# Operand addresses of a full-rate matmul: activation halves at 192 or 64 bytes from the weights, modulo 256

## What is computed

```python
def swiglu(h, w_gate_up, w_down):
    gate, up = jnp.split(h @ w_gate_up, 2, axis=-1)
    return (jax.nn.silu(gate) * up) @ w_down

def ffn_sublayer(h, shift, scale, gate, g, w_in, w_out):
    hn = modulate(rmsnorm(h, g), shift, scale)
    a, b = jnp.split(hn @ w_in, 2, axis=-1)
    y = (jax.nn.silu(a) * b) @ w_out
    return h + 0.5 * gate[:, None, :] * y
```

## Time and profile before

| | us |
|---|---|
| median of three runs | 1629.48 (1628.14 to 1629.67) |
| the profiled execution | 1628.01 |
| its span, first to last instruction | 1626.2 |
| PE busy in the span | 1593.3 (98%) |
| DVE busy | 1041.7 (64%) |
| ACT busy | 826.4 (51%) |

### The profile page before, as it was taken

How to read it: one execution, slowest core, us unless ns; L and a number is a source line. 1 busy time by engine, 2 the same in 40 slices (tenths; PEclk the granted TensorE clock), 3 DMA queues, 4 the chain that set the end, 5 groups by cost and what they waited for, 6 DMA issues and landing times.

```text
span 1626.2 us, 24165 instructions
## 1 busy us (share of the span) xinstructions
PE 1593.3 (98%) x10017; PEld 1403.6 (86%) x10017; DVE 1041.7 (64%) x1705; ACT 826.4 (51%) x1191; POOL 153.2 (9%) x141
## 2 busy tenths in 40 slices
PE   7999999999999999999999999999999999999998
PEld 6878888887889988888899999889888888789986
DVE  5786766655645577776665666557747876655554
ACT  4565544443569854444354464444544546354442
POOL 2220010100002200101001100001000000101000
PEclk9999999999999999999999999999999999999999
DMA  9756867777663365556555576598663565575552
GB/s 330 244 200 228 272 217 229 248 251 246 220 209 106 126 195 183 185 198 212 181 182 181 183 153 184 182 181 175 137 158 64 137 171 172 188 252 179 182 190 78
DMA packets 224412, 309.31 MB, mean 190 GB/s; under 512 B 5004, under 2 KB 146720, under 8 KB 224304
## 3 DMA queue, kind: packets, MB, share of 16 engines
q1 hardware_dynamic: 222208, 301.48, 60.8%
q0 software_dynamic: 1664, 5.84, 1.1%
q10 hardware_dynamic: 432, 0.45, 0.1%
HBM read 306.71 MB, written 1.05 MB: 189 GB/s over the span
## 4 chain that ended last, share of the span: by engine, by line
PE 86%; DVE 8%; ACT 4%; issue 2%; DMA 1%; ACTq 0%; DVEq 0%
PE ps L137 84%; DVE wl L150 3%; PE ps L140 2%; DVE SM L160 1%; DVE MT L160 1%; ACT wh L146 1%; ACT L146 1%; ACT SA L147 1%; ACT SA L146 1%; DMA raw<-in_a_w_qkv_dram 0%; ACT FT L146 0%; DVE MT L157 0%; DMA X<-in_x_dram 0%; DVE X L160 0%; DVE MT L150 0%
## 5 line engine op out<-in xcount | busy, mean ns | idle before, releaser
L150 DVE TENSOR_TENSOR wl<-raw,wh 128x1024 fp32r<-128x1024 f32 x498 | 611.8, 1268 | 378.7 <-ACT wh L146 378.1
L146 ACT ACTIVATE wh<-raw 128x1024 fp32r<-128x1024 f32 x498 | 501.4, 1052 | 200.9 <-PE ps L137 111.5
L137 PE MATMUL ps<-XT,wh 128*128 128x256 f32 (+1 forms) x2496 | 570.6, 315 | 2.7 <-issue 1.9
L137 PE MATMUL ps<-XT,wl 128*128 128x256 f32 x1600 | 449.0, 281 | 1.4 <-DVE wl L150 1.4
L137 PEld LDWEIGHTS ps<-XT,wh 128*128 128x128 f32 x2496 | 408.5, 189 | 43.4 <-issue 10.8
L137 PEld LDWEIGHTS ps<-XT,wl 128*128 128x128 f32 x1600 | 301.9, 189 | 2.3 <-DVE wl L150 2.0
L137 PE MATMUL ps<-wh,XR 128*128 128x512 f32 x640 | 200.5, 394 | 0.0
L137 PE MATMUL ps<-XU,wh 128*128 128x256 f32 x832 | 149.6, 282 | 0.9 <-issue 0.5
L137 PEld LDWEIGHTS ps<-wh,XR 128*128 128x128 f32 x640 | 119.6, 188 | 24.9 <-issue 0.5
L137 PE MATMUL ps<-wh,HTH 128*128 128x512 f32 x352 | 137.4, 390 | 0.0
L137 PE MATMUL ps<-wl,HTH 128*128 128x512 f32 x352 | 137.0, 389 | 0.0
(11 more groups left out here) (304 smaller groups left out, 1855.6 us busy)
## 6 DMA issues: line engine op xcount, KB each, us to landing
raw<-in_w_ffn_in_dram SPq DMA_DIRECT2D x66, 1024.0 KB, 5.1
raw<-in_ffn_w_gate_up_dram SPq DMA_DIRECT2D x44, 1024.0 KB, 5.2
raw<-in_w_in_dram SPq DMA_DIRECT2D x40, 1024.0 KB, 8.4
raw<-in_w_ada_dram SPq DMA_DIRECT2D x36, 1024.0 KB, 6.2
raw<-in_w_ffn_out_dram SPq DMA_DIRECT2D x30, 1024.0 KB, 5.0
raw<-in_ffn_w_down_dram SPq DMA_DIRECT2D x20, 1024.0 KB, 5.0
raw<-in_a_w_qkv_dram SPq DMA_DIRECT2D x12, 1024.0 KB, 7.3
raw<-in_kv_w_dram SPq DMA_DIRECT2D x8, 1024.0 KB, 6.2
```

Source lines behind the costliest of these rows:

```text
L137: return NOTHING if self.e is None else self.e.matmul(o, l, r, start=start, stop=stop, skip_group_check=skip)
L146: return self.e.activation(o, i, fn, bias=bias, scale=scale)
L150: return NOTHING if self.e is None else self.e.tensor_tensor(o, a, b, f)
```

## The change

No instruction is added, taken away or moved. Each activation gets a tile of its own over the same two regions (`XP[name]`, read through `head(name)` for H and `tail(name)` for L), with an offset by how it is used: 192 where it streams at all (`h0`, `f0`, `hk`, `hq`, `f1`, `e`, `hm`, `l`, `c1`, `c2`), 64 where it is only loaded (`ha`, `ho`, `hh`, `hb`, `hw`). `HTH`/`HTL` and `HCH`/`HCL` move from 0 to 64. The weights stay at 0. Behind the first region everything moves by 96 bytes: `C` from 64 to 160, `MT` to `SG` and the attention tiles from 128 to 224; `XC` moves from 160 to 0.

```diff
-        XR = at("XR", [P, 2, 8, T], xt0, F32R)
-        XT = at("XT", [P, 2, 8, T], xt0 + 160, F32R)
-        XRH, XRL = XR[:, 0, :, :], XR[:, 1, :, :]
-        XTH, XTL = XT[:, 0, :, :], XT[:, 1, :, :]
-        fixed.o += 2 * 8 * T * 4 + 160
+        MAIN_AT = dict(h0=192, ha=64, f0=192, hk=192, hq=192, ho=64, f1=192, e=192, hm=192, hh=64, l=192)
+        CTX_AT = dict(c1=192, c2=192, hb=64, hw=64)
+        XP = {n: at("XP" + n, [P, 2, 8, T], xt0 + d, F32R) for n, d in MAIN_AT.items()}
+        fixed.o += 2 * 8 * T * 4 + 256
...
-        f_ = Region(r0 + 384, r1)
+        f_ = Region(r0 + 352, r1)
         HTH = f_("HTH", [P, NF, T], F32R)
         HTL = f_("HTL", [P, NF, T], F32R)
...
-        XU = at("XU", [P, 2, 8, T], c_.o, F32R)
-        XV = at("XV", [P, 2, 8, T], c_.o + 352, F32R)
-        XUH, XUL = XU[:, 0, :, :], XU[:, 1, :, :]
-        XVH, XVL = XV[:, 0, :, :], XV[:, 1, :, :]
-        c_.o += 2 * 8 * T * 4 + 352
+        XP.update({n: at("XP" + n, [P, 2, 8, T], c_.o + d, F32R) for n, d in CTX_AT.items()})
+
+        def head(n):
+            return XP[n][:, 0, :, :]
+
+        def tail(n):
+            return XP[n][:, 1, :, :]
+
+        c_.o += 2 * 8 * T * 4 + 256
         r2 = c_.o
+        c_.o += 64
         HCH = c_("HCH", [P, 8, T], F32R)
         HCL = c_("HCL", [P, 8, T], F32R)
...
-                to_halves("ha", XRH, XRL, const(AB[:, 33:34]))
+                to_halves("ha", head("ha"), tail("ha"), const(AB[:, 33:34]))
```

More of the change, by code:

```diff
@@ L799, in block2_ffn @@
                 own_first[0] = False
-                for q, _ in enumerate(hidden(n, w_in, XTH, XTL, half_ready(n), range(11))):
+                for q, _ in enumerate(hidden(n, w_in, head(n), tail(n), half_ready(n), range(11))):
                     if q in GATE_PE:
@@ L905, in main @@
                 yield None
-                values = rows("av", wqkv, 2048, XTH, XTL, 8, half_ready("h0"), lambda t, n0: (a_out, "av", t, n0))
+                values = rows("av", wqkv, 2048, head("h0"), tail("h0"), 8, half_ready("h0"), lambda t, n0: (a_out, "av", t, n0))
                 tick = iter(A_TICKS)
@@ L917, in main @@
                     else:
-                        stationary(("aqk", step), wqkv, 256 * step, XTH, XTL, half_ready("h0"))
+                        stationary(("aqk", step), wqkv, 256 * step, head("h0"), tail("h0"), half_ready("h0"))
                         give(("aqk", step), a_out, "aqk", step)
@@ L924, in main @@
                 yield "gap", 1
-                for q, _ in enumerate(rows("aw", I["a_w_o"][0], 0, XRH, XRL, 8, half_ready("ha"))):
+                for q, _ in enumerate(rows("aw", I["a_w_o"][0], 0, head("ha"), tail("ha"), 8, half_ready("ha"))):
                     yield 0
@@ L931, in main @@
                 for i in range(4):
-                    stationary(("bk", i), I["kv_w"], 256 * i, XRH, XRL, half_ready("hk"))
+                    stationary(("bk", i), I["kv_w"], 256 * i, head("hk"), tail("hk"), half_ready("hk"))
                     give(("bk", i), a_out, "bk", i)
                     yield 0
-                for q, _ in enumerate(rows("bv", I["kv_w"], 1024, XRH, XRL, 8, half_ready("hk"),
+                for q, _ in enumerate(rows("bv", I["kv_w"], 1024, head("hk"), tail("hk"), 8, half_ready("hk"),
                                            lambda t, n0: (a_out, "bv", t, n0))):
@@ L948, in main @@
                     else:
-                        stationary(("bq", step), I["b_w_q"][0], 256 * step, XTH, XTL, half_ready("hq"))
+                        stationary(("bq", step), I["b_w_q"][0], 256 * step, head("hq"), tail("hq"), half_ready("hq"))
                         give(("bq", step), a_out, "bq", step)
@@ L953, in main @@
                 yield "gap", 1
-                yield from rows("bw", I["b_w_o"][0], 0, XRH, XRL, 8, half_ready("ho"))
+                yield from rows("bw", I["b_w_o"][0], 0, head("ho"), tail("ho"), 8, half_ready("ho"))
                 yield from norm_steps("gap", 2)
@@ L960, in main @@
                 yield "gap", 1
-                for _ in conv_feats("cq", 0, XRH, XRL, half_ready("hm")):
+                for _ in conv_feats("cq", 0, head("hm"), tail("hm"), half_ready("hm")):
                     yield "side", "end"
                 krows = lambda i: mkT[:, 2 * i:2 * i + 2, :].rearrange("p k t -> p (k t)")
-                for _ in conv_feats("ck", 1024, XRH, XRL, half_ready("hm"), krows):
+                for _ in conv_feats("ck", 1024, head("hm"), tail("hm"), half_ready("hm"), krows):
                     yield "side", "end"
-                for q, _ in enumerate(rows("mv", win, 2048, XRH, XRL, 8, half_ready("hm"),
+                for q, _ in enumerate(rows("mv", win, 2048, head("hm"), tail("hm"), 8, half_ready("hm"),
                                            lambda t, n0: (a_out, "mv", t, n0))):
@@ L971, in main @@
                 yield "drain"
-                gg = gates("mg", XRH, XRL, half_ready("hm"), MT[0])
+                gg = gates("mg", head("hm"), tail("hm"), half_ready("hm"), MT[0])
                 next(gg)
-                side = rows("vv", win, 5136, XRH, XRL, 8, half_ready("hm"), lambda t, n0: (a_out, "vv", t, n0))
-                side2 = rows("uu", win, 4112, XRH, XRL, 8, half_ready("hm"), lambda t, n0: (a_out, "uu", t, n0))
+                side = rows("vv", win, 5136, head("hm"), tail("hm"), 8, half_ready("hm"), lambda t, n0: (a_out, "vv", t, n0))
+                side2 = rows("uu", win, 4112, head("hm"), tail("hm"), 8, half_ready("hm"), lambda t, n0: (a_out, "uu", t, n0))
                 for _ in side:
@@ L994, in main @@
                         yield 0
-                for _ in rows("oo", win, 3088, XRH, XRL, 8, half_ready("hm"), lambda t, n0: (a_out, "oo", t, n0)):
+                for _ in rows("oo", win, 3088, head("hm"), tail("hm"), 8, half_ready("hm"), lambda t, n0: (a_out, "oo", t, n0)):
                     yield 0
@@ L998, in main @@
                 for n, n0 in (("ga", 6160), ("gb", 7184)):
-                    for q, _ in enumerate(rows(n, win, n0, XRH, XRL, 8, half_ready("hm"),
+                    for q, _ in enumerate(rows(n, win, n0, head("hm"), tail("hm"), 8, half_ready("hm"),
                                                lambda t, n0: (a_out, n, t, n0))):
@@ L1005, in main @@
                         yield 0
-                gb = rows("lb", I["w_branch_b_2"][0], 0, XVH, XVL, 8, half_ready("hb"),
+                gb = rows("lb", I["w_branch_b_2"][0], 0, head("hb"), tail("hb"), 8, half_ready("hb"),
                           lambda t, n0: (v_out, "lb", t, n0))
@@ L1013, in main @@
                     yield 0
-                for q, _ in enumerate(rows("la", I["w_branch_a_2"][0], 0, XRH, XRL, 8, half_ready("hh"),
+                for q, _ in enumerate(rows("la", I["w_branch_a_2"][0], 0, head("hh"), tail("hh"), 8, half_ready("hh"),
                                            lambda t, n0: (v_out, "la", t, n0))):
@@ L1023, in main @@
                 plan = [(512, list(range(4))), (0, list(range(4, 8))), (512, list(range(4, 8)))]
-                for _ in by_tile("lo", I["w_out_2"][0], plan, o, XVH, XVL, 8, half_ready("hw")):
+                for _ in by_tile("lo", I["w_out_2"][0], plan, o, head("hw"), tail("hw"), 8, half_ready("hw")):
                     yield 0
@@ L1071, in ctx_main @@
                     n = f"d{h0}"
-                    for q, _ in enumerate(hidden(n, I["w_ffn1_in_2"][0], XUH, XUL, half_ready("c1"),
+                    for q, _ in enumerate(hidden(n, I["w_ffn1_in_2"][0], head("c1"), tail("c1"), half_ready("c1"),
                                                  range(h0 // 2, h1 // 2))):
@@ L1085, in ctx_main @@
                 yield 0
-                yield from gates("cg", XUH, XUL, half_ready("c2"), FT[0])
+                yield from gates("cg", head("c2"), tail("c2"), half_ready("c2"), FT[0])
                 crows = lambda i: FT[i % 2][:, :]
-                yield from conv_feats("cc", 1024, XUH, XUL, half_ready("c2"), crows)
+                yield from conv_feats("cc", 1024, head("c2"), tail("c2"), half_ready("c2"), crows)
                 to_rows("cc", 3, crows(3))
                 yield 0
-                yield from rows("cv", win, 2048, XUH, XUL, 8, half_ready("c2"), lambda t, n0: (a_out, "cv", t, n0))
+                yield from rows("cv", win, 2048, head("c2"), tail("c2"), 8, half_ready("c2"), lambda t, n0: (a_out, "cv", t, n0))
                 for s in range(2):
@@ L1461, in spatial @@
                 yield
-                to_halves("hb", XVH)
+                to_halves("hb", head("hb"))
                 yield
@@ L1467, in block1_ffn @@
                 yield from normed("n" + n, X, YF, small(S_MAIN, 16), v_norm.at("bw" if layer else "aw", "x", 1))
-                to_halves(n, XTH, gain("ffn_pre_g", 8 * layer))
+                to_halves(n, head(n), gain("ffn_pre_g", 8 * layer))
                 yield
@@ L1506, in main @@
                 yield
-                to_halves("h0", XTH, gain("mix_pre_g"))
```

(39 more changed lines are left out.)

6 lines of the change are left out of this document (3 added, 3 removed).

## The result

The changed kernel takes 1633.27 us against 1628.94 us (medians of 13 runs each): ratio 1.0024, 95% interval 1.0016 to 1.0033. It is slower by a little, where 1597 us had been forecast.

A forecast was written before the change was run, and what follows sets the result against it. TensorE was taken as the bound, busy 1593.3 of 1626.2 us. The terms summed to 36.5 us less, 32.1 after 12% off for stretches paced by DVE and ACT, giving 1597 us; range 1570 to 1650.

The forecast's parts named there:

- one curve over D: All full-load matmuls: extra time over the floor depends only on D, streamed minus loaded offset modulo 256; 4.1 to 4.3 ns at 192.
- The hump: Extra against distance around the 256-byte circle: one peak near 96, its low between 160 and 256, opposite point 224.
- (a): Paired f0 and f1, 704 pairs, distance 160 to 192: 346.6 to 333.3 ns each, 9.4 us less.
- (b): Other 256-column matmuls in XT and XU, 3936, distance 160 to 192: 4.0 ns less each, 15.7 us less.
- a grid of 16 columns: Steps at multiples of 64 are whole numbers of 16 columns, so distance 192 gives 113.3 and 220.0 ns; chance 0.40.
- (c): hk and hm streaming, 576 matmuls, distance 0 to 192: 6.7 ns less each, 3.9 us less.
- (d): Halves only loaded, moved to 64, 1800 matmuls, distance 0 to 192: 6.7 ns less each, 12.0 us less.
- (e): Halves at 192 that are loaded too: 672 matmuls to 233.3 ns, 4.5 us lost; nothing for another 192 (av, cv).
- As bad as 96: Rival for all moved matmuls: distance 192 gives 126.7 and 233.3 ns, 67 us more, 1696 us; chance 0.13.
- like 0: Rival for all moved matmuls: distance 192 gives 120.0 and 226.7 ns, 15.1 us more, 1645 us; chance 0.15.
- the four signs: Timeline steps expected: last feed-forward 113.3 ns, pairs 333.3, HTH rows 220.0, row products on hm 233.3.
- the first stays over 118: Failure test: last feed-forward's 256-column step, then 117.3 ns, staying over 118 fails the forecast whatever the others do.

The follow-up runs named there:

- small_tiles: Changed kernel with every activation half back at 160 or 0, hidden ones at 0, leaving only the small tiles moved: 1627.27 us, 0.9996 of the kernel before.
- streams_192: As `small_tiles`, but the 256-column streams at 192, pairs still at 160, only-loaded halves at 0: 1616.99 us, 0.9929 of the kernel before.
- unpaired_192: `streams_192` with f0 and f1 at 192 and no longer paired, H and L streaming as two 256-column matmuls: 1617.16 us, ratio 0.9932.

## Why the prediction was wrong

- **The step that failed**: "The extra doesn't grow with the streamed length, so it comes once for each matmul and its load", and from it one curve over D for every width. The ground for it was that 256 and 512 columns have the same extra at D = 0, 10.8 and 11.0 ns. They do, but at D = 0 alone. The rows of before already spoke against it, without the run: on one curve a pair at D = 160 is 215.7 + 109.2 and 8.1 twice, 341.1 ns, and the earlier trace rows has 346.6, an extra of 10.9 for each of its two matmuls. The hump that was drawn through 96 and 160 joined a point of the 512-column curve to one of the 256-column curve. There is no single hump either: at 256 columns 224, which was to be its low, gives 118.3, while 32 gives 116.7. At 256 columns and D = 160 the extra is about 8, at 96 it is 10.8 and not 17.6; at 512 columns nearly every place but 0 is as bad as 96. The extra at 512 columns is 11 at D = 0, 13.4 at 64 and about 17.6 elsewhere, D = 192 included. The floors of 109.2 and 215.7, taken from plain float32, were reached at no place that was tried with a full load of fp32r: the least mean steps are 113.3 and 226.7.
- **(a)** forecast 9.4 us less, measured 704 x (353.2 - 346.7) = 4.6 more; alone 3.9 us more. The pair was treated as 512 and 256 columns, each on the one curve.
- **(b)** forecast 15.7 less at 113.3. Mean steps of 113.4 (`l`) to 114.9 (`hq`) in the changed kernel against 117.7 (`XU`) and 117.9 (`XT`) before: about 14 less. The size came out, but that 113.3 was hit is in part luck. The place was picked by the single hump, and the number by a grid of 16 columns for multiples of 64; both fail elsewhere. 64 and 192 themselves also stand at 117.8, which is no multiple of 16 columns, and 128 gives 118.6 to 119.1.
- **(c)** forecast 3.9 less; 576 x (119.9 - 115.7) = 2.4 less.
- **(d)** forecast 12.0 less, measured 1800 x 6.4 = 11.5 more; alone 0.6%, about 10 us. This term has the largest error, 23.5 us.
- **(e)** forecast 4.5 more for the 672; at 229.1 against 227.3 it is 1.2 more, and `av`, `cv` gain half a us.
- **What does not reach the end.** 12% was taken off. Summed over all start-to-start distances of the profiled executions, from `small_tiles` to the changed kernel the 256-column streams go from 538.9 to 523.9 us, the pairs from 244.6 to 249.2, the row products from 601.8 to 613.0, and everything else, where the waits are, from 220.9 to 224.8: 4.7 us more together, for 4.8 of the span. Of the 3.9 at the end about 1.2 is a stretch of 3.4 us at half clock (1224.8 us) that the profile of `small_tiles` doesn't have. From `small_tiles` to `streams_192` the streams win 14.9 and everything else loses 2.9, a fifth; 2.1 of it lie between 1110 and 1163, the context scan. (The 14.9 holds up to 1.7 us, an estimate, from a like stretch at half clock at 1428.0 that only `small_tiles` has.) The loss shows in the chain that ended last of `small_tiles` and of `streams_192` (start us, us, what):

```profile
1116.59 0.90 ACT FT L146 x2
1124.38 0.90 ACT FT L146 x2
1132.17 0.90 ACT FT L146 x2
```

```profile
1108.86 0.90 ACT FT L146 x2
1116.64 0.90 ACT FT L146 x2
1124.43 0.90 ACT FT L146 x2
```

  The period is 7.79 us in both, although its 48 streamed matmuls of `hm` are cheaper, 115.8 against 119.8 ns: there the chain through ACT and DVE sets the pace, as the earlier trace rows suggested for 1110 to 1163.
- **Small tiles at nothing**: right (0.9996).
- **The rivals.** "As bad as 96" (1696) described one part, the row products, which really went to 233.3; "like 0" (1645) described none. None of them let the widths differ, and so none had gains and losses of like size. The range, 1570 to 1650, holds 1633 by its breadth alone, not by its mechanism; the forecast of a clear gain was wrong. Of the four signs that were named beforehand only the first came, 113.3. The one picked out as decisive, "the first stays over 118", didn't come either, and the forecast failed all the same: one kind of matmul couldn't vouch for the others.

That the operands' places matter at all is borne out. The Trainium skill's rule (TensorE: Matmul & The Clock Gate, "Step-by-step: what each phase is for") that a load for the next matmul doesn't steal from the running one stands against 226.7 and 233.3 ns for the same matmul with its loaded operand 64 bytes further on; the measurement decides. What the two reads do to each other no profile shows; only the steps are seen.

Why a 512-column stream has another curve was not tried. By the slope of the earlier trace rows, 112 columns in 94 ns, a load of 128 columns reads for about 107 ns (an estimate): nearly all of a 256-column matmul and half of a 512-column one. That would fit two different bounds, but no run separates them. Nor was a single stretch of 512 activation columns streamed over loaded weights.

## What to carry over

Before points of several kinds of instruction are put on one curve, see whether one kind alone has two points that say the same; an agreement at a single place, here at 0, is no proof that the kinds agree. A layout number belongs to a pair of operands and to the width of the stream: measure it by kind, and give each kind its own place, which can be done in one kernel when each activation has its own tile. The simplest version that beats both kernels is `streams_192` (`unpaired_192` does as well): streams of 256 columns at 192, pairs at 160, what is only loaded at 0, 1616.99 us (ratio 0.9929).

## What had not been expected of the hardware

- Two steady steps for one instruction stream: at distance 192, and at 64 as well, 256 columns run at 113.3 ns or at 117.8. Which of the two it is stands after the first dozen matmuls of a run (begun after a transpose, a row product or a wait), and it holds until the run is broken off: in a run of 336 of `l` at 113.3 in `streams_192`, in 1056 of `f1` at 117.8 in `unpaired_192`. In the changed kernel `e` has runs of both. The lower step is the commoner one at 192, where it holds in about two thirds of the stretches of twelve over all runs; streamed at 64 it is rare. What picks it was not found. If all stood at 113.3, the 1536 matmuls of `f0` and `f1` that stand at 117.8 in `unpaired_192` would take 1536 x 4.5 = 7 us less (an estimate).
- The mean steps 113.3, 120.0, 226.7 and 233.3 ns are 272, 288, 544 and 560 columns at 2.4 GHz, but the single steps need not be even. They are at 0 (120 each; 226 or 227 each). At 96 they go round between 116 and 125 for a mean of 120.0, and nearly all halves loaded from 128 step by 228 to 241 for a mean of 232.3 to 233.3.
- Over a 512-column stream, moving the loaded operand by 32 bytes either way from 0 costs about 6.4 ns a matmul (226.9 to 233.3), as much as all places but 96 (234.2) and 192 (229.1) do.
